# A hybrid decoder layer with 64 experts: rounded passes in half of the down product, and work moved between stages

## What is computed

```python
def rwkv7_time_mix(pb, mu, ...):
    prev = jnp.pad(pb[:, :-1], ((0, 0), (1, 0), (0, 0)))
    p = pb + (prev - pb) * mu
...
def expert_block(args):
    tok, e = args
    xb = xt[tok]
    hb = jax.nn.silu(xb @ w1[e]) * (xb @ w3[e])
    return hb @ w2[e]
```

## Time and profile before

| | us |
|---|---|
| median of three runs | 2201.63 |
| the three runs | 2195.73, 2201.63, 2204.43 |
| time of the profiled execution | 2203.79 |
| span of its trace | 2201.9 |
| attention, share of the span | 144.7 |
| RWKV | 340.7 |
| router | 278.3 |
| experts | 1043.7 |
| finish | 41.9 |

### The profile page before, as it was taken

One profiled execution on the slowest core, in us unless ns is written; L12 is line 12 of the kernel. 1 busy time (PEld: TensorE's weight loads), 2 busy tenths in 40 slices (PEclk: granted clock), 3 DMA queues, 4 the chain that ended last, 5 costly groups with the idle time before them and its releaser, 6 DMA issues. The chain is left out here.

```text
span 2201.9 us, 31398 instructions
## 1 busy us (share of the span) xinstructions
PE 1914.4 (87%) x8693; PEld 1370.3 (62%) x8694; DVE 1318.8 (60%) x2399; ACT 1014.6 (46%) x1850; POOL 460.2 (21%) x336
## 2 busy tenths in 40 slices
PE   2999998773878878899869999999999999999992
PEld 2788875552777764444446676766666766666661
DVE  6567614874677753433446666666666766666675
ACT  3422214762434422222245566666566655656663
POOL 0000000003121100213412333333222332232330
PEclk9999999995989988899979999999999999999996
DMA  9055202003100009231158988989989998899965
GB/s 354 22 205 208 83 3 75 16 18 154 39 25 22 6 8 357 81 81 46 50 188 238 311 269 231 288 269 329 292 238 299 335 319 257 240 290 299 317 176 172
DMA packets 129923, 396.86 MB, mean 180 GB/s; under 512 B 22724, under 2 KB 35101, under 8 KB 126766
## 3 DMA queue, kind: packets, MB, share of 16 engines
q1 hardware_dynamic: 97134, 292.82, 37.0%
q0 software_dynamic: 32720, 103.16, 19.4%
HBM read 337.72 MB, written 77.94 MB: 189 GB/s over the span
## 5 line engine op out<-in xcount | busy, mean ns | idle before, releaser
L2030 DVE TENSOR_TENSOR w_low<-w_experts,w_high 128x1024 fp32r<-128x1024 f32 x392 | 454.4, 1221 | 130.5 <-ACT w_high L1992 111.2
L1992 ACT CAST w_high<-w_experts 128x1024 fp32r x392 | 381.9, 1046 | 51.5 <-issue 50.2
L2106 PE MATMUL ps_y<-w_experts,actT 128*128 x768 | 353.0, 603 | 23.3 <-issue 16.0
L2083 PE MATMUL ps_h<-w_high,xT_high 128*128 128x512 f32 x776 | 315.2, 406 | 5.6 <-DVE xT_low L2036 5.6
L2083 PE MATMUL ps_h<-w_low,xT_high 128*128 128x512 f32 x776 | 306.6, 395 | 0.0
L2083 PE MATMUL ps_h<-w_high,xT_low 128*128 128x512 f32 x776 | 306.5, 395 | 0.0
L1973 POOL DMA_INDIRECT acc<-y_rows,scatter_idx x96 | 152.7, 1591 | 688.8 <-DVE idx L2023 370.2
L2106 PEld LDWEIGHTS ps_y<-w_experts,actT 128*128 128x128 f32 x768 | 140.2, 193 | 168.7 <-issue 168.6
L2014 ACT COPY y_rows<-ps_y 128x512 f32<-128x512 f32 x96 | 56.4, 587 | 267.0 <-PE ps_y L2106 264.6
L1955 POOL DMA_INDIRECT gathered<-h,idx x99 | 165.3, 1670 | 47.4 <-issue 29.7
L2083 PEld LDWEIGHTS ps_h<-w_high,xT_high 128*128 128x128 f32 x776 | 146.6, 189 | 38.3 <-DVE xT_low L2036 3.8
(11 more groups left out here) (412 smaller groups left out, 3184.9 us busy)
## 6 DMA issues: line engine op xcount, KB each, us to landing
w_experts<-in_exp_w SPq DMA_DIRECT2D x384, 512.0 KB
qT<-in_w_ada POOLq DMA_DIRECT2D x16, 1024.0 KB, 5.2
w_raw<-in_w_in SPq DMA_DIRECT2D x24, 512.0 KB, 7.1
w_ada<-in_w_ada SPq DMA_DIRECT2D x8, 1024.0 KB, 11.8
acc<-y_shared SPq DMA_DIRECT2D x9, 512.0 KB, 7.5
pb<-pb_tile SPq DMA_DIRECT2D x16, 256.0 KB, 2.6
pb_cur<-pb SPq DMA_DIRECT2D x8, 512.0 KB, 3.8
pb_prev<-pb SPq DMA_DIRECT2D x8, 512.0 KB, 4.8
```

What stands on the lines that cost most here:

```text
L1992: act.copy(w13_s[par][0][:, which, k], w13[:, bass.ds(w, 1), which, k].squeeze(1)).then_inc(w_high, 1)
L2030: dve.tensor_tensor(w13_s[par][1][:, which, k], w13[:, bass.ds(w, 1), which, k].squeeze(1), w13_s[par][0][:, which, k], ALU.subtract).then ...
L2083: q = pe.matmul(ps_h[:].rearrange("p (a n) -> p a n", a=2), xT[a][:, k, :], w13_s[par][z][:, :, k, :], start=(k == 0 and m == 0), stop=(k ...
L2106: q = pe.matmul(ps_y[n][:], aT[:, k, :], w2[:, bass.ds(w, 1), k, n * BANK:(n + 1) * BANK].squeeze(1), start=(k == 0), stop=(k == FC - 1))
```

## The change

**Attention and RWKV.** SP loads chunks 0 and 1 at the front of attention, POOL mixes them there with three operations each, and RWKV begins with `lr_arguments(0)`. The mixing of chunks 2 to 7 stays as it was.

```diff
@@ attend, POOL
+            for c in range(2):
+                pool.wait_ge(pb_first[c], 32)
+                step.then(tt(before[c][:], before[c][:], mixed[c][:], ALU.subtract))
+                step.then(tt(before[c][:], before[c][:], keep["rwkv"]["mu"][:], ALU.mult))
+                step.then(tt(mixed[c][:], mixed[c][:], before[c][:], ALU.add))
@@ rwkv, POOL
-            mix(0)
             for c in range(-1, NT):
-                if here(c + 2):
+                if c >= 0 and here(c + 2):
                     mix(c + 2)
```

```diff
@@ norm_route, SP
-            for out in (*x2_out, *h2_out, *acc_out):
+            for out in (*x2_out, *h2_out):
                 sp.wait_ge(out, nth(NT))
@@ norm_route, POOL, at its end
+            for n in range(3):
+                pool.wait_ge(idx_ready, n + 1)
+                pool.indirect_dma_start(keep["xg"][n][:], None, dr["h2"], bass.IndirectOffsetOnAxis(ap=idx[n][:], axis=0),
...
@@ experts, ACT
+            act.wait_ge(acc_out[0], 8 * NT)
             split(0, 0)
             x_copy(0)
+            act.wait_ge(acc_out[1], 8 * NT)
             split(1, 1)
```

```diff
+            def split_down(n):
+                e, w = entry(act, 0, n, E - 1), entry(act, 1, n, SLOTS - 1)
+                act.wait_ge(w2_ready, e + 1)
+                act.wait_ge(dn_mm, n + 1)
+                act.copy(w2_s[0][:], w2[:, bass.ds(w, 1), 0, :].squeeze(1)).then_inc(w2_high, 1)
...
+                        split_down(b)
                         split(b + 2, j % 2)
...
-                        dve.tensor_copy(aT[:], ps_a[:, 0:F].rearrange("p (k n) -> p k n", k=FC)).then_inc(aT_ready, 1)
+                        dve.tensor_copy(aT_s[0][:], ps_a[:, 0:P]).then_inc(aT_high, 1)
+                        dve.tensor_copy(aT[:], ps_a[:, P:2 * P])
+                        dve.wait_ge(aT_high, b + 1)
+                        dve.tensor_tensor(aT_s[1][:], ps_a[:, 0:P], aT_s[0][:], ALU.subtract).then_inc(aT_ready, 1)
+                        w = entry(dve, 1, b, SLOTS - 1)
+                        dve.wait_ge(w2_high, b + 1)
+                        dve.tensor_tensor(w2_s[1][:], w2[:, bass.ds(w, 1), 0, :].squeeze(1), w2_s[0][:], ALU.subtract).then_inc(w2_low, 1)
                         dve.wait_ge(y_free, b + 1)
...
                         for n in range(2):
-                            for k in range(FC):
-                                q = pe.matmul(ps_y[n][:], aT[:, k, :], w2[:, bass.ds(w, 1), k, n * BANK:(n + 1) * BANK].squeeze(1),
-                                              start=(k == 0), stop=(k == FC - 1))
+                            pe.matmul(ps_y[n][:], aT[:], w2[:, bass.ds(w, 1), 1, n * BANK:(n + 1) * BANK].squeeze(1), start=True, stop=False)
+                        pe.wait_ge(w2_low, b + 1)
+                        for n in range(2):
+                            for m, (a, z) in enumerate(PASSES):
+                                q = pe.matmul(ps_y[n][:], aT_s[a][:], w2_s[z][:, n * BANK:(n + 1) * BANK], start=False, stop=(m == 2))
```

More of the change, by code:

```diff
@@ L539, in _ @@
             sp.dma_start(dr["pb"][0:1, :], zero[:]).then_inc(keep["rwkv_in"], 16)
+            sp.wait_ge(keep["rwkv_in"], 16 * 16)
+            for c in range(2):
+                sp.dma_start(mixed[c][:], dr["pb"][c * P + 1:(c + 1) * P + 1, :]).then_inc(pb_first[c], 16)
+                sp.dma_start(before[c][:], dr["pb"][c * P:(c + 1) * P, :]).then_inc(pb_first[c], 16)
             for i, (h, n) in enumerate(ITEMS):
@@ L738, in rwkv @@
         chunk = [Chunk(sb, j) for j in range(2)]
-        mixed = [sb(f"p_mixed{j}", [P, B_COLS]) for j in range(4)]
+        mixed = keep["mixed"]
+        assert nc.sbuf_base <= MIXED_AT
+        sb("p_mixed", [P, (MIXED_AT - nc.sbuf_base) // 4 + 4 * B_COLS])
         gate = [sb(f"gate{j}", [P, BW]) for j in range(3)]
@@ L1722, in block_rows, with first_rows @@
                 step.then(dve.tensor_copy(lists[:, P:NB], empty[:].to_broadcast([P, NB - P])))
+            def first_rows():
+                dve.wait_ge(rows_T, 1)
+                step.then(dve.tensor_copy(lists[:, 0:P], ps_c[:, 0:P]))
+                for j in range(4):
+                    dve.tensor_copy(idx[j][:], lists[:, j:j + 1]).then_inc(idx_ready, 1)
             for r in range(-1, NT + 2):
@@ L1865, in _ @@
                 if r >= 2:
+                    up(r - 2, 1)
+                if r < NT:
+                    transpose_h(r)
+                if 1 <= r < NT:
+                    place(r - 1)
+                if r < NT:
+                    route(r)
+                if r == NT + 1:
+                    pe.wait_ge(rows_in, 16)
+                    pe.transpose(ps_c[:, 0:P], list_rows[:], ident[:]).then_inc(rows_T, 1)
+                if r >= 2:
+                    transpose_act(r - 2)
+                if r == NT:
+                    pe.wait_ge(sched_sums, 1)
+                    mm(ps_b[0:E, 0:1], upper[0:E, 0:E], nblk[:], start=True, stop=True).then_inc(sched_mm, 1)
+                if r >= 2:
                     down(r - 2)
-            pe.wait_ge(rows_in, 16)
-            pe.transpose(ps_c[:, 0:P], list_rows[:], ident[:]).then_inc(rows_T, 1)
 def experts(nc, io, dr, keep):
@@ L1956, in gather @@
                                          bounds_check=S - 1, oob_is_err=False).then_inc(xg_in[j], 16)
-            for n in range(3):
-                gather(n, n)
+            for j in range(2):
+                pool.wait_ge(acc_out[j], 8 * NT)
             with pool.Fori(0, TURNS) as i:
```

113 lines of the change are left out of this document (63 added, 50 removed).

## The result

The changed kernel takes 2265.6 us in the median (2254.4 to 2269.7), the kernel before 2203.0 beside it: a ratio of 1.029, with a 95% interval of 1.025 to 1.033. It is slower, as forecast, but by 63 us where 18 were forecast, and outside the stated range. The profiled execution took 2261.7 us, its span is 2259.9, against 2203.8 and 2201.9 before.

A forecast was written before the change was run, and what follows sets the result against it. It took a two-block loop through ScalarE, VectorE and TensorE to replace TensorE as the experts' bound. Experts +35, RWKV's start and attention -10.4, router -7: +18 on 2203.8 is 2221.4, against the median 2220 us; range 2190 to 2246.

The forecast's parts named there:

- TensorE's share of down: Experts, down product: four of 8 halves replaced by six passes, 3.43 to 3.12 us, 0.31 less per block; block 9.84 by PE alone.
- The loop: Experts: copy, down weights' cast and subtraction, low part, up(b+2), down(b+1), copy; 19.4 becomes 21.3 us for two blocks, becoming the bound.
- + 0.50 x 95 = +47: Experts: blocks lengthen from 10.15 to 10.65 us over 95 blocks, costing 47 us.
- I take 12 away: Experts: of today's 43 us of waits, 12 vanish in PE's new slack of 0.8 us per block; bounds 0 and 43.
- the sum of the stage, +35: Experts stage in all: +35 us, from +4 to +47.
- rival 3: More is paid: VectorE held up by POOL (+9), longer hand-overs (+14) or late weights; about +25, 2245 us; chance 0.16.
- Attention: Attention: six POOL mixing operations moved in, 14 us mostly hidden, may delay VectorE; +5 us, bounds 0 and 14.
- RWKV's start: RWKV's start: ScalarE begins near 500.9 instead of 515.22, -14.3, and an addition goes, -1.1; together -15.4 us.
- Router: Router to experts: stage ends 2.7 us sooner, gathered rows ready, first up product -9.2, lists +2; net -7, from -3 to -9.
- The second: PE stays the bound in the experts: blocks of 9.84 us, -29 there, -47 in all, 2155 us; chance 0.13.
- The first: The waits swallow it: 36 to 43 of 43 us of experts' waits disappear in PE's slack; 2188 to 2195 us; chance 0.17.

The follow-up runs named there:

- the control: Four extra fp32r products per block on TensorE, on top of the moved pair, where TensorE has few gaps: 2220.8 us.
- the extra products: Changed kernel plus fp32r products per block on TensorE, before its wait for the low part, into an unread bank: four 2230.7 us, two 2235.4 us.
- the moved pair: Changed kernel with the down weights' cast and subtraction moved behind the second of four pieces of the next up weights: 2188.9 us, ratio 0.994.
- both schedules: Changed kernel without its down part (down in fp32 as before); earlier mixing in attention and the router's new order stay: 2195.9 us, ratio 0.996.

## Why the prediction was right in sign and wrong in size

**TensorE's share of down: right.** Down takes from 1510.29 to about 1513.40, 3.11 us, for 3.12 forecast; a block without gap or spell is 9.85 us, for 9.84.

**The loop: right as a mechanism, and its length that of the shortest case.** 21.3 us for two blocks were forecast; 19 of the 61 pairs without a spell are under 21.5, and half are at 21.8 or more. VectorE's subtraction of the down weights starts 2.6 us after ScalarE's copy of the result in the block shown (1516.28 against 1513.65), for 2.5, 2.7 in the median and up to 4.1. The 1.42 us from copy to cast were read from one block of before, and a quarter of that kernel's blocks take 1.9. Taking some 1 us out of the loop of two blocks at either of two places, 48 us by itself, gave 77 and 79 us back, because the spells went with it.

**The step that failed: "+ 0.50 x 95 = +47 ... I take 12 away", the sum of the stage, +35.** It treats a gap on TensorE as costing its own length. From the first up product to the last, 96 distances of 11.235 us against 10.605 are +60.5. The loop at its shortest is + 0.52 x 96 = +50. The spells cost 28 us (26.4 in the up products, 1.7 in a down of 4.81 us instead of 3.11) against 7 before (1.7 in the first up product, 5.1 in three downs), so +21. The remainder is -11, for the 12 taken away; in it old waits that went into the slack and the loop's longer pairs stand together, and no run parts them. The missing term is the low clock: in the forecast no price stood for what follows a gap, and rival 3 named hand-overs and late weights, not this. The stages of before held a hint, a granted clock of 0.99 in the experts, where TensorE is hardly ever idle, and 0.93 in attention, where it is. Filling the gaps took out all spells but the first, and 28 us of the stretch with them, 35 of the median; the control shows that nothing else in the extra products helps.

**Attention: the size was off within its bounds.** +5 was taken between 0 and 14, and +10.8 measured: 7.1 us of VectorE's waits for POOL, the rest beside a lower granted clock in the stage (0.89 for 0.93). Three of the eleven profiles with this code show a clock of 0.91 to 0.92 there, and take 153.6 to 153.9 us instead of 157.2, so the lower clock goes with 3.5 of the 10.8 us. I had left it open whether operations that read PSUM wait; they don't, but four of those that don't read it ran into a POOL operation, and TensorE's gaps grew.

**RWKV's start: right.** -15.4 forecast, -13.3 measured, with the first activation 14.2 us earlier within the stage.

**Router: right, for a partly wrong reason.** -7 forecast, -5.1 measured. "The stage ends some 2.7 us sooner" without the wait for the last write of `acc` did not happen: the last copy ends at 1116.48 and the next stage's first DMA is issued at 1119.86, 3.4 us later, as before (3.4). Taking that wait away gained nothing; what the 3.4 us are was not tried. And of the way to the first up product, VectorE's four subtractions (4.63 us from 1122.93) stand ahead of the low part of the rows and were left out. The gain comes from the gathered rows that are there: from the first cast to the first up product are 7.2 us, 13.1 before.

**Rivals.** The second (TensorE stays the bound) fell, for the reason given. What it needed, under 0.9 us added to the loop, is not even reached by the moved pair, which adds 1.2. The first fell too: the remainder above is 11 us, not 36 to 43. The third had the size of its effect, the attention part, and a longer hand-over, which the traces show in every fourth block (0.5 us at ScalarE's cast), but not the clock.

Of the 45 us between forecast and result, 25 are the experts, 6 attention, 2 RWKV and 2 the router; the rest is the projection's 5 and the place of the profiled execution, which lies 4 us under its median where that of before lay above.

## What to carry to other kernels

Before giving the busiest engine less work at the cost of two others, write down the loop that leads through all of them and its slack: here 96% busy on TensorE stood beside a loop with 0.9 us to spare, and the 2.2 us added in a row cost more than they freed. Where they must be added, put them where the slower of the two engines is the only one on the path. And a gap on TensorE may cost more than its length, so an edit that makes a full engine wait now and then needs a second price, for the clock. A slow operand read in front of a product of the engine that sets the pace was worth 14 us with one line moved, twice what both schedules gained, but only in the kernel where that engine sets the pace.

## What the runs showed of the hardware that was not expected

- Gaps of 0.88 and 0.70 us on TensorE, 1.6 us in a stretch of 10, were followed by eight passes at a granted clock of 0.50. Gaps of 1.41 and 0.69 us in the distance from 1720.35 to 1732.81 were not, so the length of the gaps doesn't decide it alone; what else does was not tried. Extra products of 0.47 us per block were enough to make all spells but the first vanish, though 35 us of gaps stayed.
- A 128x1 operation on VectorE, 0.22 us by itself, took 2.33 beside a POOL operation of 2.34 us.
- A read of a table entry in SBUF into a register of TensorE takes 0.31 us in the median but up to 1.64, 25 times in 192, and at most 0.39 when it stood in front of the up product. Why the place matters was not tried.
- A stage's end costs 3.4 us from the last copy to the next stage's first DMA, with the wait for the last write of `acc` and without.
